# A fused attention and gated-delta layer in fp32: block layouts for the inputs, five modulation pieces, a new prologue and new orders

## The reference, cut to what matters

```python
mod = silu(c) @ ada_w + ada_b                    # 1024 x 3072
shift, scale, gate = split(mod, 3)
h = rmsnorm(x, pre_norm_w) * (1 + scale) + shift
proj = h @ w_in                                  # 1024 x 4104
mq, mk, mv, mg, dq, dk, dv, dz, db, da = split(proj)
o_moba = causal_attention(rope(mq), rope(mk), mv) * silu(mg)      # 8 heads of 64
dq, dk, dv = silu(causal_conv4(dq, dk, dv))                       # 4 heads of 128
g = -exp(a_log) * softplus(da + dt_bias); beta = sigmoid(db)
o_dn = rmsnorm(gated_delta_rule(dq, dk, dv, g, beta), dn_norm_w) * silu(dz)
y = concat(o_moba, o_dn) @ w_out
out = x + gate * rmsnorm(y, post_norm_w)
```

## Time and profile before

| | us |
|---|---|
| median of 3 runs | 208.96 (208.71 to 212.08) |
| profiled execution, own time | 208.55 |
| its span | 206.5 |
| PE busy in the span | 186.6 |
| DVE / ACT / POOL busy | 127.0 / 105.9 / 96.5 |
| bytes moved | 38.39 MB, mean 186 GB/s |

### The profile page before, as it was taken

One profiled execution on the slowest core, in us unless ns is written; L12 is line 12 of the kernel. 1 busy time (PEld: TensorE's weight loads), 2 busy tenths in 40 slices (PEclk: granted clock), 3 DMA queues, 4 the chain that ended last, 5 costly groups with the idle time before them and its releaser, 6 DMA issues.

```text
span 206.5 us, 4647 instructions
## 1 busy us (share of the span) xinstructions
PE 186.6 (90%) x1863; PEld 171.6 (83%) x1863; DVE 127.0 (61%) x306; ACT 105.9 (51%) x197; POOL 96.5 (47%) x51
## 2 busy tenths in 40 slices
PE   0079999999999989999999999999999999999980
PEld 0078999999999879999988999898999787788860
DVE  0634977752169988988586852677795135963055
ACT  4735573546476499965650445335251465545230
POOL 2003385687984927978642039701800480045400
PEclk9999999999999999999999999999999999999997
DMA  6999999994760587289247802450890094020022
GB/s 229 347 362 357 386 357 367 369 383 117 253 205 4 159 171 207 76 124 285 62 109 242 299 12 51 159 205 3 301 396 22 16 312 183 18 83 0 3 102 102
DMA packets 27881, 38.39 MB, mean 186 GB/s; under 512 B 2818, under 2 KB 21459, under 8 KB 27860
## 3 DMA queue, kind: packets, MB, share of 16 engines
q1 hardware_dynamic: 27572, 37.05, 55.6%
q10 hardware_dynamic: 288, 1.05, 1.4%
HBM read 37.04 MB, written 1.05 MB: 185 GB/s over the span
## 4 chain that ended last, share of the span: by engine, by line
PE 80%; DVE 10%; DMA 3%; SPq 2%; ACT 1%; issue 1%; POOL 1%; DVEq 0%; POOLq 0%
PE bank L1243 18%; PE bank L1245 16%; PE bank L1244 16%; DVE cv L886 6%; PE bank L1444 3%; DMA ada<-in_ada_w 3%; PE bank L1455 3%; PE bank L1432 2%; PE bank L1273 2%; PE bank L1266 2%; PE bank L1550 2%; PE bank L1526 2%; PE bank L1492 1%; SPq L322 1%; PE bank L1557 1%; PE bank L1503 1%
## 5 line engine op out<-in xcount | busy, mean ns | idle before, releaser
L442 POOL TENSOR_TENSOR wlo<-raw,whi 128x1024 fp32r<-128x1024 f32 (+1 forms) x30 | 69.6, 2338 | 75.7 <-ACT whi L520 75.7
L1243 PE MATMUL bank<-hhi,whi 128*128 128x256 f32 x224 | 66.0, 295 | 0.5 <-DVE hlo L837 0.5
L1244 PE MATMUL bank<-hhi,wlo 128*128 128x256 f32 x224 | 64.5, 288 | 0.0
L1245 PE MATMUL bank<-hlo,whi 128*128 128x256 f32 x224 | 64.5, 288 | 0.0
L1243 PEld LDWEIGHTS bank<-hhi,whi 128*128 128x128 f32 x224 | 44.1, 197 | 1.7 <-DVE hlo L837 0.9
L1244 PEld LDWEIGHTS bank<-hhi,wlo 128*128 128x128 f32 x224 | 44.2, 197 | 0.0
L1245 PEld LDWEIGHTS bank<-hlo,whi 128*128 128x128 f32 x224 | 44.0, 197 | 0.0
L520 ACT ACTIVATE whi<-raw 128x1024 fp32r<-128x1024 f32 (+1 forms) x33 | 32.8, 1026 | 15.7 <-DMA raw<-in_w_in 12.1
L886 DVE SCALAR_TENSOR_TENSOR cv<-bank,convh,cv 128x255 f32<-128x255 f32 (+2 forms) x36 | 17.0, 481 | 6.6 <-ACT cv L566 5.5
L865 DVE SCALAR_TENSOR_TENSOR bank<-ada,sml,bank 128x512 f32<-128x512 f32 x22 | 16.6, 753 | 0.6
L1243 PE MATMUL bank<-whi,ohi 128*128 128x512 f32 x32 | 12.8, 400 | 0.0
(11 more groups left out here) (195 smaller groups left out, 348.8 us busy)
## 6 DMA issues: line engine op xcount, KB each, us to landing
raw<-in_w_in SPq DMA_DIRECT2D x20, 512.0 KB, 8.0
ada<-in_ada_w SPq DMA_DIRECT2D x32, 256.0 KB, 7.8
ada<-in_ada_w SPq DMA_DIRECT2D x4, 1024.0 KB, 12.0
raw<-in_w_out SPq DMA_DIRECT2D x8, 512.0 KB, 4.8
raw<-in_w_in SPq DMA_DIRECT2D x5, 384.0 KB, 7.3
qkvs<-in_w_in SPq DMA_DIRECT2D x4, 384.0 KB, 8.0
cv<-in_w_in SPq DMA_DIRECT2D x4, 384.0 KB, 8.6
xs<-in_x ACTq DMA_DIRECT2D x2, 512.0 KB, 3.9
```

The costliest lines, as they stand in the source:

```text
L442: pool.tensor_tensor(split_u(wlo, n), raw_u(n), split_u(whi, n).bitcast(F32), ALU.subtract).then_inc(lo_done, 1)
L1243: pe.matmul(out, a[0][ia], b[0][ib], start=start, stop=False, skip_group_check=skip)
L1244: pe.matmul(out, a[1][ia], b[0][ib], start=False, stop=False, skip_group_check=skip)
L1245: return pe.matmul(out, a[0][ia], b[1][ib], start=False, stop=stop, skip_group_check=skip)
```

## The change

Everything that the host passes in is laid out anew (`layouts`): ada_w as 5 pieces, each partition's share contiguous; w_in's units likewise; all vectors (also dt_bias and a_log, broadcast) as 89 columns in front of the constants, in one array. The modulation has the pieces `PIECES = [(0, 1), (1, 1), (2, 2), (4, 2), (6, 2)]` (first k, number of k): two of 256 columns, then three of 512. In piece 0 DVE sums input blocks 0 and 1 and PE the six others. PE runs 13 matmuls of constants (`busy`, 256 columns, fp32, results never read) in the prologue. DVE squares and scales one half of x. The lists of all engines are in new orders. What is computed is the same.

```diff
+PIECES = [(0, 1), (1, 1), (2, 2), (4, 2), (6, 2)]
...
-        DVE_K = (6, 8, 8, 8)
+        DVE_K = (2, 8, 8, 8, 8)
+        XT_BANK = (5, 4, 3, 2)
...
-        DVE_LO = (2, 38, 40)
+        DVE_LO = (41, 42, 43)
...
+            def load_front():
+                sp.dma_start(cst[:, 0:C_COS], const[:, 0:C_COS]).then_inc(front_loaded, 16)
+                sp.dma_start(xs[:, 1, :], x[0, P:, :]).then_inc(x_loaded[1], 16)
+
+            def load_ada(p, g0, g1):
+
+                k0, n = PIECES[p]
+                if p == 3 and g0 == 0:
+                    sp.wait_ge(acc_done, 2)
+                    sp.wait_ge(direct_done, NK - DVE_K[0])
+                if p == 4 and g0 == 0:
+                    sp.wait_ge(acc_done, 3)
+                for g in range(g0, g1):
+                    o = NK * k0 * 256 + g * n * 512
+                    sp.dma_start(ada_piece(p)[:, 2 * g:2 * g + 2, :].rearrange("p k n -> p (k n)"),
+                                 ada[:, o:o + n * 512]).then_inc(ada_ready(p, 2 * g)[0], 16)
...
-                sp.dma_start(dab[:, 0:4], dt_bias[0].partition_broadcast(P)).then_inc(dab_loaded, 16)
-                sp.dma_start(dab[:, 4:8], a_log[0].partition_broadcast(P)).then_inc(dab_loaded, 16)
-                sp.dma_start(wba[:, :, :], w_in[0, :, DBA:DBA + 8].rearrange("(k p) n -> p k n", p=P)).then_inc(wba_loaded, 16)
+                sp.dma_start(wba[:, :, :], w_gates[:, :, :]).then_inc(wba_loaded, 16)
...
+            def modulated(p):
+
+                k0, n = PIECES[p]
+                act.wait_ge(mod_read, p + 1)
+                if p == 0:
+                    act.wait_ge(xT_ready, 1)
+                else:
+                    act.wait_ge(xT_done[k0 // 2], 1)
...
-            def mod_sums(q, k0, k1):
-
-                a = bank[6 + q % 2][:, :]
-                if q == 1 and k0 == 0:
+            def mod_sums(p, k0, k1):
+
+                n = 256 * PIECES[p][1]
+                a = bank[6 + p % 2][:, 0:n]
+                if p == 1 and k0 == 0:
                     dve.wait_ge(mod_read, 1)
...
+                dve.tensor_tensor(mod_b[:, k2], b[:, 0:n], pcol[:, R_SHIFT + k0:R_SHIFT + k0 + n], ALU.add)
+                for k in range(k0, k0 + n):
+                    ins = dve.scalar_tensor_tensor(mod_a[:, k:k + 1], b[:, n + k - k0:n + k - k0 + 1], scale1[:, k:k + 1],
+                                                   pcol[:, R_PRE + k:R_PRE + k + 1], ALU.add, ALU.mult)
...
-            gates_in()
             conv_silu(0)
             conv_silu(1)
+            gates_in()
             rope(0)
+            conv_silu(2)
             gates_out()
-            conv_silu(2)
...
-            pe.transpose(bank[7][:, 0:NROWS], prow[0:NROWS, :], ident[0:NROWS, 0:NROWS]).then_inc(prow_turned, 1)
+            def busy(b, n):
+
+                pe.wait_ge(ones_set, 1)
+                for _ in range(n):
+                    pe.matmul(bank[b][:, 0:256], ones[:, :], ones[:, 0:1].to_broadcast([P, 256]), start=True, stop=True)
...
             def qkv_products(n):
 
                 k = n // 2
-                pe.wait_ge(hlo_done, k // 2 + 1)
+                pe.wait_ge(hlo_done, piece_of(k) + 1)
...
+            busy(1, 3)
+            busy(3, 8)
+            mod_direct(2)
+            mod_direct(3)
+            busy(2, 1)
+            mod_direct(4)
+            mod(0)
+            mod_direct(5)
+            busy(0, 1)
             mod_direct(6)
             mod_direct(7)
             x_turn(0)
-            mod(0)
...
             k_turn(0)
+            cum()
             k_turn(1)
-            cum()
```

More of the change, by code:

```diff
@@ L460, in _ @@
             lo(1)
+            lo(2)
             lo(3)
@@ L1625, in _ @@
             qkv_products(5)
-            mod(2)
+            mod(3)
             qkv_products(6)
@@ L1779, in constants, with layouts, columns, across @@
         c[:, C_LV + l * HALF:C_LV + (l + 1) * HALF] = (m // (2 * b) == q // (2 * b)) & (m // b % 2 == 0)
-    return c
-_INS = ["x", "c", "ada_w", "ada_b", "pre_norm_w", "post_norm_w", "w_in", "conv_w", "a_log", "dt_bias", "dn_norm_w", "w_out"]
+    return c[:, NROWS:]
+def layouts(x, c, ada_w, ada_b, pre_norm_w, post_norm_w, w_in, conv_w, a_log, dt_bias, dn_norm_w, w_out):
+    def columns(a):
+        return a.reshape(-1, P).T
+    def across(a):
+        return np.broadcast_to(a.reshape(1, -1), (P, a.size))
+    front = [columns(c), columns(ada_b[:, 0:2 * D]), columns(pre_norm_w), columns(dn_norm_w), columns(conv_w), across(dt_bias), across(a_log)]
+    rows = ada_w[0].reshape(NK, P, 3, D)
+    pieces = [rows[:, :, 0:2, k0 * P:(k0 + n) * P].transpose(1, 0, 2, 3).reshape(P, -1) for k0, n in PIECES]
+    gate = [rows[:, :, 2, i * 512:(i + 1) * 512].transpose(1, 0, 2).reshape(P, -1) for i in range(2)]
+    w = w_in[0].reshape(NK, P, -1)
+    rest = [w[4 * hf:4 * hf + 4, :, g:g + 256].transpose(1, 0, 2).reshape(P, 1, -1) for g in GROUPS for hf in range(2)]
+    return {"x": x, "ada": np.concatenate(pieces, 1), "gate_w": np.concatenate(gate, 1), "gate_b": ada_b[:, 2 * D:], "post_norm_w": post_norm_w,
+            "w_qkv": w[:, :, DQ:DQ + 3 * DW].transpose(1, 0, 2).reshape(P, N1, HQ), "w_rest": np.concatenate(rest, 1),
+            "w_gates": w[:, :, DBA:DBA + 8].transpose(1, 0, 2), "w_out": w_out, "const": np.concatenate(front + [constants()], 1)}
 def kernel(**inputs):
```

606 lines of the change are left out of this document (317 added, 289 removed).

## The result

| | before | after |
|---|---|---|
| median, lowest and highest (us) | 208.84, 208.33 to 212.08, 4 runs | 202.07, 202.01 to 202.14, 4 runs |
| ratio of the times | | 0.9684, 95% interval 0.9665 to 0.9703 |
| profiled execution, its span (us) | 208.55, 206.5 | 202.14, 200.2 |

The change makes the kernel 3.2% faster. The ratio leaves out the one run of 212.08, in which the chip was in a slower state. The forecast was 205.1. "Faster", which had 0.42, came true against 0.52 for "within 2%".

The account below looks back on a forecast made before the run. PE was taken to bound the kernel, busy 186.6 of 206.5 us. From the profiled 208.55, 2.9 for the earlier qkv end and 0.6 at the gates gave 205.05, stated as 205.1; range 202.2 to 208.6.

Parts of the forecast that it names:

- The start: PE's prologue: fillers, direct matmuls and coefficients put the first qkv product at 15.75 us, 5.3 earlier, and at the fast clock.
- the two splits: DVE's splits for k = 1 and for k = 2 and 3 during the qkv products, done at 22.8 and 30.05 us.
- E: The moment the qkv products end and `ba` starts: 60.74 us before, forecast 57.85, 2.9 earlier.
- DVE's path: Before the first qkv product: coefficients, four sums and a split on DVE, with signals, take 3.05 us.
- two waits for `hlo`: Behind the first qkv product PE waits 2.3 and 2.1 us for DVE's splits, 4.4 in all.
- Rival B: Behind its start PE doesn't wait for DVE, or much less: 200.7 us in full, 202.9 for half; chance 0.17.
- F: New orders wait somewhere unseen, or POOL's lower parts come late in the last qkv units: +1 to +4, 207.5; chance 0.10.
- the fast clock: Fillers raise PE's clock early, so the first qkv products run at 0.12 instead of 0.21 us each, worth 2.5.
- Rival C: PE's clock falls back between fillers and first products: 210.2 or 206 us, together about 207.5; chance 0.16.
- The gates' sums: Between E and q's turns: the small gate instruction, now later, no longer waits for POOL; 0.6 us gained, else 0.7 lost.
- later orders: bounds 0 and +1.5, I take 0: Halves, attention, inverse and w_out products: same instructions in new orders, so no gain and at most 1.5 us lost.
- the transfers are worth nothing by themselves: Start: computed work covers the loads at 349 or 400 GB/s, so layout gains nothing; without cover, at most 5 us.

Follow-up runs that it names:

- no_fill: The changed kernel without its 13 filler matmuls: 203.69 us, ratio 0.9793 to the kernel before.
- layout_back: The changed kernel without its layout: ada_w and w_in read from the arrays as given, ada_w in twice as many transfers: 216.77 us, ratio 1.044 to before.
- mid0: The changed kernel without the two fillers between the one-column matmuls of the start, the eleven ahead kept: 201.33 us, ratio 0.9679 to before.
- experiment 3: The kernel before with only ada_w and w_in in blocks contiguous per partition: 206.27 us, ratio 0.9896.
- experiment 1: The changed kernel with the old orders on all engines from ba and the first convolution on, and for later loads: 203.98 us, ratio 0.9814 to before.
- orders_back: Same run as experiment 1: the changed kernel with the old orders behind the qkv products, 203.98 us.
- layout_only: Same run as experiment 3: the kernel before with only the new layout of ada_w and w_in, 206.27 us.
- fill_turns: The changed kernel with three more fillers, behind the first three blocks of x's turns: 203.60 us, ratio 0.9773 to before.
- direct1: The changed kernel with four input blocks of the second modulation piece summed on PE instead of DVE: 201.40 us, ratio 0.9671 to before.
- both: The changed kernel with the edits of mid0 and direct1 together: 201.16 us, ratio 0.9676 to before.
- Experiment 10: The changed kernel with PE's halves 14, 13, 15 set apart and pv(3) put between q(2) and q(3): 213.52 us, ratio 1.0243 to before.
- experiment 11: The changed kernel with two PE swaps, scores(0) ahead of half(7) and p_turn(3) between halves 18 and 17: 210.22 us, ratio 1.0103 to before.
- orders_only: The kernel before with only the new orders from ba and the first convolution on, and for later loads: 220.95 us, four scattered runs.
- layout_orders: The kernel before with the new layout of ada_w and w_in and the new later orders, old prologue and four pieces: 205.77 us, ratio 0.9875.

## Why the prediction was right, and where it failed

**The start was right, with one term missing.** First product 15.26 for 15.75, the two splits within 0.2, E within 0.3. The fillers and one-column matmuls were done 0.7 earlier than I said (12.01 for 12.7). DVE's path took 2.84 us from the coefficients (12.24) to the first split (15.08), for my 3.05. But it was not quite what set the first product: PE had no idle time in front of it, since x's turns, for which the sum had no term, kept it busy at half speed from 12.01 to 15.26. Behind the first product I had two waits for `hlo`, of 2.3 and 2.1. PE waited 1.9 up to the first of those splits and 1.7 more up to the second, but for four things: `hlo` (0.29 and 1.11), DVE's sums (0.58 and 0.61) and ACT's copy of x (1.07), which I had not listed. Rival B, that PE would not wait for DVE, falls, though its 202.9 is nearer to the measured time than the forecast is; that is chance. (The "E" at the end of the prediction's chances is no rival; F was meant.)

**The reason for the fast clock was not.** I gave the fillers the fast products. `no_fill` shows that those are fast without them; the fillers' 1.6 us is in the one-column matmuls. Rival C came true in that the clock fell (0.50 over the turns) and not in its price: the 0.95 that I had put on the fall was too much, since E came 0.3 later than in the sum that left it out. The Trainium skill, "TensorE: Matmul & The Clock Gate", "Part 4: PE-mode transpose", says that transposes don't count as busy. The fall in the changed kernel fits that, but other runs of this case don't: in `layout_back` the clock fell ahead of the turns, which start at 12.92, so that the last eight records of one-column matmuls took 1.68 us instead of 0.95,

```profile
11.38 1.68 PE L1336 MATMUL bank<-sml,ada 128*128 128x1 f32 x8
```

in `mid0` it fell 0.07 us ahead of them, and in `no_fill` it rose while they ran. So the turns are not shown to cause the fall; the one-column matmuls ahead of them are a rival that nothing here rules out.

**The gates' sums were right in size, wrong in cause.** 0.9 gained for 0.6. The stall went because the transfer behind it came in time (experiment 3: 1.26 us at the gates with the old orders), not because the new order put the instruction later. By itself the new order costs 0.6 there (experiment 1).

**The step "later orders: bounds 0 and +1.5, I take 0" failed**, and is the miss of 3 us. "Same count, same shapes" was true and did not give the same time. The stretch to the last matmul is 120.6 to 120.9 in the three kernels with the old orders (before, `orders_back`, `layout_only`) and 118.1 in six with the new ones in which nothing waits (after, `no_fill`, `fill_turns`, `mid0`, `direct1`, `both`), whatever the start and the layout are. Start to start, by kind of work, the old orders with the new start against the change: halves and output products 69.96 to 69.32 (fifteen rows of them became nine), gate sums 2.1 to 1.5, q 3.0 to 2.7, vnew 3.0 to 2.7, kk 2.15 to 1.95, v's turns 1.0 to 0.9, z 4.9 to 4.75; some others changed by 0.1 either way. Two of these can be seen in rows. Before:

```profile
167.21 1.09 PE L1503 MATMUL bank<-state,qd 128*64 128x128 f32 x8
...
171.79 1.13 PE L1577 MATMUL bank<-accg,ones 128*128 128x512 f32 x2
```

After:

```profile
162.64 0.27 PE L1561 MATMUL bank<-state,wT 128*64 128x128 f32 x1
162.70 0.27 PE L1572 MATMUL bank<-state,qd 128*64 128x128 f32 x1
...
165.49 1.74 PE L1572 MATMUL bank<-state,qd 128*64 128x128 f32 x16
...
170.54 1.13 PE L1646 MATMUL bank<-accg,ones 128*128 128x512 f32 x2
171.11 0.80 PE L1305 MATMUL bank<-whi,ohi 128*128 128x512 f32 x1
```

Two groups of small products that follow each other and write to different halves of the partitions (64 columns of stationary data each) run into one another: `vnew(2)` and `q(1)` alternate in the trace, and sixteen q products take 1.57 where eight took 1.0. Experiment 10 took one such neighbour away and lost 0.23 of it: this is the one cause that a run shows. The gate sums are in part a matter of counting. The second one stands in front of an output product and takes 0.57 from its start to the next where it took 1.05, but that next one takes 0.63 to its own next, where the first of such a row took 0.31 to 0.34 in the old order. So 0.3 of the 0.6 us only moved into the output products' figure, and the rows of halves and output products must have saved more than their 0.64, some 0.9. That each row costs something at its ends is then the largest candidate (0.15 for each of six rows), but the one swap that tests it (experiment 11) shows 0.04. So it is shown that the orders make the 2.5 us, and for one pair of neighbours how; what a row of halves costs, and why it costs 0.04 at one place and would have to cost more at others, stays open. The two kernels meant to price it broke on waits of their own.

**The step "the transfers are worth nothing by themselves" failed** too, though it doesn't show in the sum. The engines that move data were busy for 0.97 of the first 50 us before; in the earlier trace rows the share stands beside the 349 and 400, as 1.10 and 1.03, and I did not weigh it. My bound of 5 us for a lost cover was too low. It was 14.7 (in its profile, which is 0.4 above the median, 3.0 up to E, 8.5 at the gates and 3.6 behind them), since the table ordered late in the list lands late as well, DVE, which works in order, passes that on to the gates, and PE's clock falls in the wait. F, that the new orders wait, is what happens without the layout.

By parts, from the medians: layout alone -2.05, orders then -0.5 (within the noise), the new start then -3.7. Taken out of the change one at a time, they give +14.7 (layout), +1.9 (orders), +1.6 (fillers). The sums don't match because the parts need each other, which a list of terms, each against the old kernel, cannot show.

## What to carry to other kernels

An order of steps is a term of its own: the same matmuls in another order took 2% less here, by what stands next to what, and 4 to 6% more (experiments 11 and 10, against the change) when one step was late and PE's clock fell in the wait, so ask for both signs before you write zero. When a stall is traced to a busy engine, go one row further, to what made that engine late. Where the transfers' share is near 1 in a stretch, a layout is not free to ignore: price it against the schedule as it will be after the change, not as it was.

## What the runs showed that was not expected

In ten profiles with the early start PE's clock came back between 1.0 us before and 2.0 us behind the first product. In those with the old start it came 5.5 us behind it in the kernel before, 5.8 in `layout_only`, and 0.2 to 0.3 ahead of it in `orders_only` and `layout_orders`. The changed kernel's four times lie within 0.13 us, where the 4 to 14 runs of the kernel before spread over 3.4 to 5.1. That the scatter is the moment of this rise fits, and was not tested. Nor is the length of a wait all that decides how long the clock stays down behind it: behind 4.6 us (experiment 10) it read 0.50 for some 14 us of full work, behind 5.2 (experiment 11) for 3.4, behind the 1.1 at the gates in `layout_orders` for 3.4, and behind the 0.9 there in the changed kernel not at all.
